# Last out projection of each layer by token groups, with the norms counted by group

## The reference

```python
def first_block(...):
    for i in range(DEPTH):                      # 2: attention, retention
        ...
        x = layer_norm(ALPHA * x + y, ln_gain[i], ln_bias[i])

def layer_norm(x, gain, bias):
    mu = jnp.mean(x32, axis=-1, keepdims=True)
    var = jnp.mean(jnp.square(x32 - mu), axis=-1, keepdims=True)
    y = (x32 - mu) * lax.rsqrt(var + LN_EPS)
    return y * gain + bias

def second_block(...):
    h = rms_norm_2(x, norm_attn[l]) * (1.0 + sc1) + sh1
    ...
    mix = jnp.concatenate([out_a, out_b], axis=-1) @ w_out[l]
    x = x + g1 * mix
    h = rms_norm_2(x, norm_ffn[l]) * (1.0 + sc2) + sh2
    x = x + g2 * conv_ffn(h, w_up[l], conv_w[l], conv_b[l], w_down[l])
    return rms_norm_2(x, norm_final)
```

## Time and profile before

| | us |
|---|---|
| median of 3 runs | 2315.85 |
| lowest, highest | 2310.59, 2321.92 |
| profiled execution | 2316.7 |
| its span, first to last instruction | 2315.0 |
| TensorE busy | 2251.7 |
| VectorE busy | 1681.1 |
| ScalarE busy | 994.0 |
| mean granted TensorE clock | 0.996 |

### The profile page before, as it was taken

How to read it: one execution, slowest core, us unless ns; L and a number is a source line. 1 busy time by engine, 2 the same in 40 slices (tenths; PEclk the granted TensorE clock), 3 DMA queues, 4 the chain that set the end, 5 groups by cost and what they waited for, 6 DMA issues and landing times.

```text
span 2315.0 us, 29071 instructions
## 1 busy us (share of the span) xinstructions
PE 2251.7 (97%) x10804; PEld 1859.1 (80%) x10804; DVE 1681.1 (73%) x1861; ACT 994.0 (43%) x1016; POOL 137.7 (6%) x197
## 2 busy tenths in 40 slices
PE   7999999999999999999999999999999999999997
PEld 6878888887878888888787778787888888888886
DVE  5788877978877778677785676984655666665567
ACT  4443433434434434343443456454444344444443
POOL 2110010010000000000001101000000000000000
PEclk9999999999999999999999999999999999999999
DMA  7877776587777777777746645455655555555653
GB/s 254 288 263 256 254 254 218 186 322 265 272 262 271 266 254 275 256 266 263 253 144 177 212 137 164 141 168 165 191 190 183 191 188 186 193 183 184 197 182 127
DMA packets 260289, 503.59 MB, mean 218 GB/s; under 512 B 14705, under 2 KB 68385, under 8 KB 259328
## 3 DMA queue, kind: packets, MB, share of 16 engines
q1 hardware_dynamic: 228480, 381.73, 50.1%
q0 software_dynamic: 31376, 119.80, 15.0%
q10 hardware_dynamic: 368, 1.18, 0.1%
HBM read 498.90 MB, written 3.69 MB: 217 GB/s over the span
## 4 chain that ended last, share of the span: by engine, by line
PE 51%; issue 36%; DVE 6%; DMA 4%; ACT 1%; POOL 0%; SPq 0%; DVEq 0%; ACTq 0%; POOLq 0%
PE pair_t L412 15%; PE pair_t L414 15%; PE pair_t L413 15%; DMA raw<-in_attn_w_in_dram 2%; DVE w_lo L406 1%; PE sc L776 1%; PE turn L532 1%; ACT w_hi L401 1%; DVE m_acc L1026 1%; DMA raw<-in_w_in_dram 1%; PE sc L768 1%; DMA raw<-in_ret_w_in_dram 1%; PE sc L1572 1%; PE sc L640 0%; PE sc L622 0%
## 5 line engine op out<-in xcount | busy, mean ns | idle before, releaser
L406 DVE TENSOR_TENSOR w_lo<-raw,w_hi 128x2048 fp32r<-128x2048 f32 (+1 forms) x367 | 822.4, 2243 | 500.8 <-ACT w_hi L401 496.4
L401 ACT ACTIVATE w_hi<-raw 128x2048 fp32r<-128x2048 f32 (+1 forms) x367 | 689.3, 1879 | 1071.8 <-DMA raw<-in_ret_w_in_dram 351.5
L412 PE MATMUL pair_t<-w_hi,x_hi 128*128 128x512 f32 (+1 forms) x2080 | 814.2, 391 | 20.8 <-DVE w_lo L406 13.5
L414 PE MATMUL pair_t<-w_hi,x_lo 128*128 128x512 f32 (+1 forms) x2080 | 799.0, 384 | 0.0
L413 PE MATMUL pair_t<-w_lo,x_hi 128*128 128x512 f32 (+1 forms) x2080 | 798.5, 384 | 0.0
L412 PEld LDWEIGHTS pair_t<-w_hi,x_hi 128*128 128x128 f32 x2080 | 392.8, 189 | 108.9 <-DVE w_lo L406 15.8
L414 PEld LDWEIGHTS pair_t<-w_hi,x_lo 128*128 128x128 f32 x2080 | 392.4, 189 | 77.7
L413 PEld LDWEIGHTS pair_t<-w_lo,x_hi 128*128 128x128 f32 x2080 | 393.0, 189 | 72.9 <-issue 0.2
L1026 DVE SCALAR_TENSOR_TENSOR m_acc<-m_raw,csilu,m_acc 128x1024 f32<-128x1024 f32 x180 | 230.7, 1282 | 6.9 <-DMA m_raw<-in_w_mod_dram 3.5
L412 PE MATMUL pair_t<-w_hi,f_hh 128*128 128x512 f32 x352 | 138.0, 392 | 0.4 <-DVE f_y L2120 0.4
L414 PE MATMUL pair_t<-w_hi,f_hl 128*128 128x512 f32 x352 | 137.0, 389 | 0.0
(11 more groups left out here) (354 smaller groups left out, 2088.2 us busy)
## 6 DMA issues: line engine op xcount, KB each, us to landing
m_raw<-in_w_mod_dram POOLq DMA_DIRECT2D x96, 1024.0 KB, 5.9
raw<-in_ret_w_in_dram SPq DMA_DIRECT2D x192, 512.0 KB, 4.7
raw<-in_w_up_dram SPq DMA_DIRECT2D x176, 512.0 KB, 4.3
raw<-in_w_down_dram SPq DMA_DIRECT2D x88, 512.0 KB, 4.5
raw<-in_attn_w_in_dram SPq DMA_DIRECT2D x64, 512.0 KB, 4.8
raw<-in_ret_w_out_dram SPq DMA_DIRECT2D x64, 512.0 KB, 4.8
raw<-in_w_in_dram SPq DMA_DIRECT2D x56, 512.0 KB, 4.7
...
```

The source lines that it names most:

```text
L401: act.activation(chunk(w_hi, c, width), chunk(raw, c, width), ACT.Copy).then_inc(sem("hi"), 1)
L406: v.tensor_tensor(chunk(w_lo, c, width), chunk(raw, c, width), chunk(w_hi, c, width).bitcast(F32), ALU.subtract).then_inc(sem("lo"), 1)
L412: pe.matmul(to, xh, wh, start=start, stop=False)
L414: return pe.matmul(to, xl, wh, start=False, stop=stop)
```

## The change

The last out projection of each of the four layers is done in the order (c, token) = (0,0) (0,1) (1,0) (2,0) (3,0) (1,1) (2,1) (3,1), by `output_by_token`. Before (2,0) TensorE waits for both sums of chunk 0; before (3,0) for the sum of (1,0) (`b_half_read`); before (3,1) for the sum of (1,1). `products` still counts when token 1 of a chunk is done, and a new count in `b_half` tells of (1,0), (2,0) and (3,0). VectorE sums, takes statistics and normalizes token by token; the powers on GpSimd are counted by token (six instead of three, four more at the ends of the second block), so are squares and scales on ScalarE. The dummy matmuls are 12, 46 and 15 instead of 22, 71 and 28. In ScalarE's queue, chunks 1 and 2 of the next block's weights are rounded later: chunk 1 behind the first token's norm, chunk 2 behind `turn_hi` or (retention) behind the first token's scale. In the second block's feed-forward, chunk 1 is now split inside `turn_lo` and chunk 2 behind it. The stores go out token by token.

```diff
                     behind[j]()
+        HALF_DONE = {"a": 0, "r": 3, "b0": 6, "b": 10, "f": 13}
+        HALF_READ = {"a": 1, "r": 2, "b0": 2, "b": 7, "f": 8}
+        TOKENS = [(0, 0), (0, 1), (1, 0), (2, 0), (3, 0), (1, 1), (2, 1), (3, 1)]
+        def output_by_token(pe, b, oh, ol, before):
+            for c, t in TOKENS:
+                before(c, t)
+                if t == 0:
+                    pe.wait_ge(sem("lo"), CH * b + c + 1)
+                for k in range(CH):
+                    mm = product(pe, pair[c % 2][t][:, :], oh[:, k, t * P:(t + 1) * P],
+                                 ol[:, k, t * P:(t + 1) * P], c, k, CB, k == 0, k == CH - 1)
+                if t == 1:
+                    mm.then_inc(sem("products"), 1)
+                elif c:
+                    mm.then_inc(sem("b_half"), 1)
...
+            def before_last(c, t):
+                if c < 2 and t == 0:
+                    before(c)
+                elif (c, t) == (2, 0):
+                    pe.wait_ge(sem("a_sum_z"), 2 + 4 * (i - 1) + 1)
+                elif (c, t) == (3, 0):
+                    pe.wait_ge(sem("b_half_read"), HALF_READ["a"])
+                elif (c, t) == (3, 1):
+                    pe.wait_ge(sem("a_sum_z"), 2 + 4 * (i - 1) + 2)
+            if last:
+                output_by_token(pe, a_block(i, 0), a_oh, a_ol, before_last)
...
-            pe_fill(pe, turn[0], 22)
+            pe_fill(pe, turn[0], 12)
...
-            pe_fill(pe, turn[0], 71)
+            pe_fill(pe, turn[0], 46)
...
-            for c in range(3):
-                round_hi(act, R_B0, c)
-            act_normalize(act, 1, 1)
+            round_hi(act, R_B0, 0)
+            act_normalize(act, 0)
+            round_hi(act, R_B0, 1)
+            act_normalize(act, 1)
             turn_hi(act, 1, False)
+            round_hi(act, R_B0, 2)
...
             if which == "a":
                 vec_a_turn(v, i)
             split_lo(v, b, 3)
-            for c in range(CH):
-                vec_sum(v, which, 2 + 4 * (i - 1) + c, CH * b + c + 1, c)
-                v.wait_ge(sem(which + "_sum_z"), 2 + 4 * (i - 1) + c + 1)
-                for t in range(NT):
-                    ins = v.bn_stats(stats[:, t, c, :], z[:, t, c * CB:(c + 1) * CB])
-                vec(ins)
-                if c == 0:
-                    split_lo(v, b + 1, 0)
-            vec_wait(v)
+            base = 2 + 4 * (i - 1)
+            def stat(t, c):
+                return v.bn_stats(stats[:, t, c, :], z[:, t, c * CB:(c + 1) * CB])
+            def token_sum(t, c):
+                if t == 0:
+                    v.wait_ge(sem("b_half"), HALF_DONE[which] + c)
+                else:
+                    v.wait_ge(sem("products"), CH * b + c + 1)
+                w = slice(c * CB, (c + 1) * CB)
+                ins = v.tensor_tensor(z[:, t, w], z[:, t, w], pair[c % 2][t][:, :], ALU.add)
+                if t == 1:
+                    ins.then_inc(sem(which + "_sum_z"), 1)
+                    v.wait_ge(sem(which + "_sum_z"), base + c + 1)
+                elif c == 1:
+                    ins.then_inc(sem("b_half_read"), 1)
+                    v.wait_ge(sem("b_half_read"), HALF_READ[which])
+                else:
+                    vec(ins)
+                    vec_wait(v)
+                vec(stat(t, c))
+            def variance(t):
+                vec_wait(v)
+                vec(v.bn_aggr(mv[:, t, :], stats[:, t, :, :]))
+                vec_wait(v)
+                v.tensor_scalar(var[:, t:t + 1], mv[:, t, 1:2], LN_EPS, None, ALU.add).then_inc(sem("var"), 1)
+            def shift(t):
+                v.wait_ge(sem("rsqrt"), t + 1)
+                v.scalar_tensor_tensor(out=nmr[:, t:t + 1], in0=mv[:, t, 0:1], scalar=-1.0, in1=rstd[:, t:t + 1],
+                                       op0=ALU.mult, op1=ALU.mult).then_inc(sem("norm_stats"), 1)
+            def centred(t):
+                v.wait_ge(sem("rows_in"), 64)
+                vec(v.scalar_tensor_tensor(out=z[:, t, :], in0=z[:, t, :], scalar=mv[:, t, 0:1],
+                                           in1=rows[:, 0, :], op0=ALU.subtract, op1=ALU.mult))
+            def scaled(t):
+                vec_wait(v)
+                v.wait_ge(sem("rsqrt"), 3 + t)
+                for h in range(2):
+                    w = slice(h * D // 2, (h + 1) * D // 2)
+                    v.scalar_tensor_tensor(out=z[:, t, w], in0=z[:, t, w], scalar=rstd[:, t:t + 1],
+                                           in1=rows[:, 1, w], op0=ALU.mult, op1=ALU.add).then_inc(sem("z_full"), 1)
+            vec_sum(v, which, base, CH * b + 1, 0)
+            v.wait_ge(sem(which + "_sum_z"), base + 1)
             for t in range(NT):
-                vec(v.bn_aggr(mv[:, t, :], stats[:, t, :, :]))
-            vec_wait(v)
-            v.tensor_scalar(var[:, :], mv[:, :, 1], LN_EPS, None, ALU.add).then_inc(sem("var"), 1)
+                vec(stat(t, 0))
+            split_lo(v, b + 1, 0)
+            for c in range(1, CH):
+                token_sum(0, c)
+            variance(0)
             if which == "r":
+                centred(0)
+                token_sum(1, 1)
+                scaled(0)
+            else:
+                token_sum(1, 1)
+                shift(0)
+            for c in range(2, CH):
+                token_sum(1, c)
+            variance(1)
+            if which == "r":
+                vec_rms(v, 1, 0)
+                centred(1)
+                scaled(1)
                 return
-            v.wait_ge(sem("rsqrt"), n)
-            v.scalar_tensor_tensor(out=nmr[:, :], in0=mv[:, :, 0], scalar=-1.0, in1=rstd[:, :],
-                                   op0=ALU.mult, op1=ALU.mult).then_inc(sem("norm_stats"), 1)
-            for h in range(2):
-                zz = z[:, 1, h * 1024:(h + 1) * 1024]
-                v.tensor_scalar(zz, zz, mv[:, 1, 0:1], rstd[:, 1:2], ALU.subtract, ALU.mult)\
-                    .then_inc(sem("z_norm1"), 1)
+            shift(1)
+            zz = z[:, 1, 1024:2048]
+            v.tensor_scalar(zz, zz, mv[:, 1, 0:1], rstd[:, 1:2], ALU.subtract, ALU.mult)\
+                .then_inc(sem("z_norm1"), 1)
...
-            power(rstd[:, :], var[:, :], "var", 2, "rsqrt")
+            for t in range(NT):
+                power(rstd[:, t:t + 1], var[:, t:t + 1], "var", 3 + t, "rsqrt")
...
-            pe_fill(pe, turn[0], 28)
+            pe_fill(pe, turn[0], 15)
...
-            act_rms(act, 1)
+            act_rms(act, 1, 0)
+            round_hi(act, B_B0, 1)
+            act_scale_first(act, 1)
+            round_hi(act, B_B0, 2)
+            act_rms(act, 1, 1)
...
+            round_hi(act, B_B0 + 10, 3)
+            round_hi(act, f_block(0, 0), 0)
+            act_rms(act, 2, 0)
+            act_scale_first(act, 2)
...
+        def vec_tokens(v, which, n, counter, done, b, tmp, row, behind, weigh=None):
+            def one(t, c):
+                if t == 0 and c:
+                    v.wait_ge(sem("b_half"), HALF_DONE[which] + c)
+                else:
+                    v.wait_ge(sem("products"), CH * b + c + 1)
+                w = slice(c * CB, (c + 1) * CB)
+                ins = v.tensor_tensor(tmp[:, t, :], pair[c % 2][t][:, :], rows[:, row, w], ALU.mult)
+                if t == 1:
+                    ins.then_inc(sem(counter), 1)
+                    v.wait_ge(sem(counter), done + c + 1)
+                elif c == 1:
+                    ins.then_inc(sem("b_half_read"), 1)
+                    v.wait_ge(sem("b_half_read"), HALF_READ[which])
+                else:
+                    vec(ins)
+                    vec_wait(v)
+                ins = v.tensor_tensor(z[:, t, w], z[:, t, w], tmp[:, t, :], ALU.add)
+                if (t, c) == (0, 0):
+                    vec(ins)
+                    vec_wait(v)
+                    return
+                full = 4 + 7 * (n - 2) + FULL[c, t]
+                ins.then_inc(sem("z_full"), 1)
+                v.wait_ge(sem("z_full"), full)
+            for c, t in SQUARES:
+                one(t, c)
+                if weigh:
+                    weigh(t, c)
+                if (c, t) in behind:
+                    behind[c, t]()
...
+            split_lo(v, B_B0 + 10, 3)
+            vec_tokens(v, "b", 2, "b_scaled", 12, B_B0 + 10, b_tmp, 0,
+                       {(0, 1): lambda: split_lo(v, f_block(0, 0), 0), (1, 1): lambda: vec_rms(v, 2, 0)})
...
-            for h in range(2):
-                for t in range(NT):
+            for t in range(NT):
+                for h in range(2):
                     w = slice(h * D // 2, (h + 1) * D // 2)
-                    sp.wait_ge(sem(f"final{t}"), h + 1)
+                    sp.wait_ge(sem("final0" if t == 0 or h == 0 else "final1"), 1 if (t, h) == (1, 1) else 2 * t + h + 1)
```

233 lines of the change are left out of this document (135 added, 98 removed).

## The result

| | before | changed |
|---|---|---|
| median, us | 2316.02 (4 runs) | 2332.07 (4 runs) |
| lowest, highest | 2310.59, 2321.92 | 2329.01, 2332.96 |
| profiled execution, its span | 2316.7, 2315.0 | 2332.3, 2330.6 |
| mean granted clock | 0.996 | 0.989 |

The changed kernel is slower by a factor of 1.0058, 95% interval 1.0032 to 1.0084. The forecast was 2328.7 us; 2332.07 lies in its range.

A forecast was written before the change was run, and what follows sets the result against it. TensorE's products (97% busy) plus the gaps between them bound the kernel. Net terms 3.45 + 2.7 + 3.95 - 0.4 + 3.2 (clock) = +12.9 us on 2316.7 gave 2329.6; the median, 0.85 lower, 2328.7 us; range 2320.5 to 2333.

The forecast's parts named there:

- The new waits: Last projections of all four layers: TensorE waits for VectorE's sums at the third or fourth pass, +17.8 us together.
- a wait of 4.55: Second attention's last projection: (3,0) waits 4.55 us behind ScalarE's chunk, the next chunk's split and a gate-row product.
- The ends: Layer ends: first transposes 3.7, 14.5 and 4.3 us behind the last product, feed-forward tail 9.25; gains 2.0, 2.35, 2.95, 4.35.
- 1.6 and 3.3 us for both: Retention's end: 1.6 us less were the power free at once, 3.3 less were ScalarE's queue empty too.
- its other half: Retention's end: token 1's power, issued first, would hold VectorE's centring back some 0.6 us; left out of the sum.
- The start of the retention layer: Behind attention: chunk 2 of the next weights split at 15.1 us, wanted at 14.4 after a slow restart, +0.8 us.
- 2.35 us were forecast: Behind the second attention: rounding of the next weights comes late, 15.1 against 12.8 when products are there, +2.35 us.
- Rival (d): Next block's start: delayed transfers of chunks 1 and 2 make it wait +3 us more, 2332 us; chance 0.05.
- The clock: Three new waits over 4 us inside projections: low TensorE clock costs 1.6 us each, two of three taken, +3.2 us.
- six gaps: Earlier trace: six gaps of 3 to 5 us without products, clock low behind three and not behind three.
- (b): Last projections: clock falls at every wait, retention's two shorter ones too, +1.6 and some 1.0 more, 2331.5 us; chance 0.13.
- The third rival: Last projections: products do not wait and only the ends' gains count, 8.6 us faster, 2307 us; chance 0.05.

The follow-up runs named there:

- first variant: Changed kernel with VectorE splitting chunk 0 of the next weights behind the sum of (1,0), in attention, retention and second attention: 2326.67 us, ratio to before 1.0049.
- first_tokens: Changed kernel with only the second attention's VectorE order changed, (0,0) summed and (0,1) multiplied ahead of the split of its own chunk 3: 2333.73 us (2 runs).

## Why the prediction was right, and where it was not

The time lay 3.4 us above the forecast. As the sections below show, the waits and the ends were forecast rightly but for one place, and the closeness of the total is in part luck.

**The new waits** were right in sum (17.5 us for 17.8), and in place and cause at four of the five; the first variant removed two of them by putting the next chunk's split later. One step failed: "Second attention: (3,0) could start at 1534.16 ... a wait of 4.55". The wait is at (2,0), behind the split of the layer's own chunk 3 and two products with a gate row, 3.57 us. For retention the prediction had asked at (2,0) and (3,0); for the second attention at (3,0) only. The two variants with that layer's queue (the split moved, and `first_tokens`) settle it.

**The ends** were right to 0.8 us: 3.82, 13.79, 4.02 and 8.9 us, against 3.7, 14.5, 4.3 and 9.25. At retention the steps are those of the sum, a power beside the centring and then ScalarE's queue, and the variant that mended both gave 2.5 us; their shares (1.6 and 3.3 us for both, by the prediction) were not separated. In the changed kernel GpSimd does token 1's first power 0.1 us ahead of the centring, and the second norm's power of token 0, the one that ScalarE waits for, behind it:

```profile
1193.71 0.55 POOL L1581 TENSOR_TENSOR rstd<-var,minus_half 128x1 f32<-128x1 f32 x1 [6.62 <-DVE var L1369]
1194.22 2.31 POOL L2641 TENSOR_TENSOR rstd<-var,minus_half 128x1 f32<-128x1 f32 x1
```

```profile
1193.80 2.34 DVE L1378 SCALAR_TENSOR_TENSOR z<-z,mv,rows 128x2048 f32<-128x2048 f32 x1
```

The power that starts under the centring takes 2.31 us, four times the 0.55 of the one issued first. The centring takes 2.34, as in the earlier trace rows: it was not held back by the power ahead of it. Of the rule in the Trainium skill, "SBUF — State Buffer", section "Who interferes with whom", this case shows the half in which VectorE shuts GpSimd out; its other half cost nothing here, and leaving it out of the sum was right.

**The start of the retention layer** was too cheap: chunk 2 late by 0.8 us in the sum, 2.34 in the trace, because the products were at full clock and not slow as assumed. It then cost 1.6 us of slow steps as well. In the second attention it was the other way round: 2.35 us were forecast for products at full clock, and the trace has a wait of 0.75 us behind a restart with 1.7 us of slow steps.

**Rival (d)**, late transfers, is near in number only: ScalarE rounds chunk 2 right behind its last `x_hi`, at 424.51 us, without a wait for a transfer. It is the queue that makes that chunk late.

**The clock** is the term that was mis-sized. The prediction counted three waits of over 4 us and took two falls, +3.2 us. The profiles show 12.6 us against 1.4, +11.2: 6.0 of the 12.6 behind four of the five waits (13 slow steps behind the feed-forward's, where eight had been assumed), 6.6 at two restarts, at the late w_lo and at a gap of 3.40 us, 40 us behind retention (2.63 before). That gap ends with a ScalarE copy that stands behind a rounding, which waits for a transfer in both traces; why it is 0.8 us wider was not looked into. Without the clock the four places sum to 21.9 - 11.2 = 10.7 us, where the forecast had 9.7. The reading under this term was also too narrow: its six gaps, three of them with a low clock behind, leave out others of 3.0 to 3.6 us without such products in the trace of before (eight of 3.0 us from 489 to 1136 us, one of 3.6 ahead of 1238.9), all with the full clock behind (matmuls of other kinds run in them). Of the rivals (b) is nearest in mechanism, but it had 2.6 us more than the forecast for the clock, and 8.0 more were found. The rule cited from the Trainium skill, "TensorE: Matmul & The Clock Gate", section "What's actually happening", that half clock is the default state, would have given 4.8; the count of 19 in 23 is on its side.

**Luck in the number.** The forecast added 12.9 us. The four places cost 21.9 in the traces, 9.0 more, of which the clock is 8.0. The spans of the two traces differ by 15.6 only, since 4.5 and 1.8 us came from stretches that the change does not touch, and the medians differ by 16.05. The prediction had no term for either.

The trace of before was a quiet one in its clock, though not in its time: it took 2316.7 us, above the median, with the long form of the wait near 50 us in it. In 45 executions of before the mean granted clock ran from 0.991 (2323.6 us) to 0.997 (2311.0), with a median of 0.994; the profiled one had 0.996. Between these ends that is 2.1 us for each 0.001, and 1.8 by a straight line through all 45. So, as an estimate from these numbers, the median of before carries some 4 us of low clock that its trace does not show, and the change added that much less to the median than to the trace. The prediction took durations and clock from that one trace; this offset part of what its clock term left out.

**The third rival** (no waits, 8.6 us faster) was a fair account of the ends: with all waits removed and the rest mended the kernel gains 16 us. That took five edits together, and whether all are needed was not tested. Its deciding point, the split of the next chunk 0, was named right for the waits at (3,0) of two layers. In the second attention it is the layer's own chunk 3; for the two waits at (2,0) of retention and the feed-forward the edits moved that split and the order of the sums together.

**Open.** Why the clock falls at one gap and not at a like one is not settled, nor whether filling a wait brings it on elsewhere. What the earlier chunk 2 is worth alone was not separated from the other mends. The wait near 50 us was not looked into.
